# First shift as columns of matmuls, its weights in eight buffers, bias table first

## What is computed

```python
def ada_modulation(c, w, b):
    mod = jax.nn.silu(c) @ w + b            # c: 1024; w: 1024 x 3072
    shift, scale, gate = jnp.split(mod, 3, axis=-1)

# per sublayer m = 0..3 (attention, MLP, pooling, MLP)
h = rms_norm(x, norm_w[m]) * (1.0 + scale) + shift
x = x + gate * sublayer(h)
# attention of sublayer 0: sliding-window scores + bias = rel_bias[t5_bucket(dist)]
```

## Time and profile before

| | us |
|---|---|
| median of three runs | 957.27 (956.63 to 958.10) |
| the profiled execution's own time | 958.09 |
| its span | 956.4 |
| PE busy | 888.4 (93%) |
| DVE busy | 692.1 (72%) |
| ACT busy | 456.8 (48%) |
| first weight matmul starts | 48.44 |
| ACT takes block 0 from PE | 58.22 |

### The profile page before, as it was taken

How to read it: one execution, slowest core, us unless ns; L and a number is a source line. 1 busy time by engine, 2 the same in 40 slices (tenths; PEclk the granted TensorE clock), 3 DMA queues, 4 the chain that set the end, 5 groups by cost and what they waited for, 6 DMA issues and landing times.

```text
span 956.4 us, 17671 instructions
## 1 busy us (share of the span) xinstructions
PE 888.4 (93%) x7028; PEld 852.6 (89%) x7028; DVE 692.1 (72%) x877; ACT 456.8 (48%) x573; POOL 58.0 (6%) x104
## 2 busy tenths in 40 slices
PE   2599999899999996799999999999999999999996
PEld 1388879799999996699999999988989999999996
DVE  4889878788878888766666556855487877776665
ACT  2347464566643333456663433444465444444445
POOL 2110110211111110000000000000000000000000
PEclk9789999999999996799999999999999999999998
DMA  9895755499989994057765555653435555654531
GB/s 336 300 339 193 244 200 177 130 319 322 317 306 330 330 316 134 23 184 234 239 199 176 175 183 168 197 166 130 157 90 177 177 179 187 218 173 158 169 126 44
DMA packets 156600, 196.60 MB, mean 206 GB/s; under 512 B 5341, under 2 KB 143116, under 8 KB 156556
## 3 DMA queue, kind: packets, MB, share of 16 engines
q1 hardware_dynamic: 142732, 145.64, 47.6%
q0 software_dynamic: 13824, 50.34, 14.4%
HBM read 194.90 MB, written 1.06 MB: 205 GB/s over the span
## 4 chain that ended last, share of the span: by engine, by line
PE 81%; DVE 9%; ACT 4%; issue 2%; DMA 2%; SPq 1%; DVEq 0%; ACTq 0%
PE G L557 15%; PE G L558 15%; PE G L559 15%; PE A L557 7%; PE A L559 7%; PE A L558 7%; DVE w_lo L1123 2%; ACT w_hi L1786 2%; PE G L632 2%; PE A L685 2%; PE G L633 2%; PE G L634 2%; DMA sinks<-in_attn_sinks_dram 1%; DMA MIX<-bias_rows 1%; DVE HN L1285 1%
## 5 line engine op out<-in xcount | busy, mean ns | idle before, releaser
L1123 DVE TENSOR_TENSOR w_lo<-raw,w_hi 128x2048 fp32r<-128x2048 f32 x135 | 307.1, 2275 | 163.7 <-ACT w_hi L1786 163.5
L1786 ACT ACTIVATE w_hi<-raw 128x2048 fp32r<-128x2048 f32 x135 | 256.6, 1901 | 265.7 <-PE A L559 132.4
L557 PE MATMUL G<-h_hi,w_hi 128*128 128x256 f32 x880 | 257.9, 293 | 22.5 <-DVE h_lo L1268 13.0
L558 PE MATMUL G<-h_lo,w_hi 128*128 128x256 f32 x880 | 253.3, 288 | 0.0
L559 PE MATMUL G<-h_hi,w_lo 128*128 128x256 f32 x880 | 253.2, 288 | 0.0
L557 PEld LDWEIGHTS G<-h_hi,w_hi 128*128 128x128 f32 x880 | 173.0, 197 | 29.5 <-issue 22.5
L558 PEld LDWEIGHTS G<-h_lo,w_hi 128*128 128x128 f32 x880 | 173.6, 197 | 0.2 <-issue 0.2
L559 PEld LDWEIGHTS G<-h_hi,w_lo 128*128 128x128 f32 x880 | 173.2, 197 | 0.0
L557 PE MATMUL A<-u_hi,w_hi 128*128 128x256 f32 x512 | 143.4, 280 | 0.7 <-DVE w_lo L1123 0.7
L558 PE MATMUL A<-u_lo,w_hi 128*128 128x256 f32 x512 | 142.9, 279 | 0.0
L559 PE MATMUL A<-u_hi,w_lo 128*128 128x256 f32 x512 | 142.9, 279 | 0.0
(11 more groups left out here) (325 smaller groups left out, 1315.7 us busy)
## 6 DMA issues: line engine op xcount, KB each, us to landing
raw<-in_mlp_w_dram SPq DMA_DIRECT2D x64, 1024.0 KB, 5.5
ada_raw<-in_ada_w_dram POOLq DMA_DIRECT2D x88, 512.0 KB, 5.7
raw<-in_w_in_dram SPq DMA_DIRECT2D x14, 1024.0 KB, 5.0
raw<-in_w_up_dram SPq DMA_DIRECT2D x11, 1024.0 KB, 5.4
raw<-in_w_gate_dram SPq DMA_DIRECT2D x11, 1024.0 KB, 5.3
raw<-in_attn_w_in_dram SPq DMA_DIRECT2D x9, 1024.0 KB, 7.1
raw<-in_w_down_dram SPq DMA_DIRECT2D x8, 1024.0 KB, 5.2
raw<-in_attn_w_out_dram SPq DMA_DIRECT2D x4, 1024.0 KB, 5.4
```

Of the source, the lines that this page charges most:

```text
L557: pe.matmul(dst, wh, ah, start=start, stop=False)
L558: pe.matmul(dst, wh, al, start=False, stop=False)
L1123: dve.tensor_tensor(w_lo[n % 2][:, 0:k, :], raw[n % RAW][:, 0:k, :], w_hi[n % 2][:, 0:k, :].bitcast(F32), ALU.subtract).then_inc(lo_done, 1)
L1786: act.activation(w_hi[n % 2][:, 0:k, :], raw[n % RAW][:, 0:k, :], ACT.Copy).then_inc(hi_done, 1)
```

## The change

The shift's weights of sublayer 0 no longer go through DVE. POOL loads them into eight buffers that the opening doesn't use otherwise (`shift_w`), in between and behind the scale's; PE multiplies each 128 x 128 tile by a column of silu(c) and accumulates over the eight k-tiles in one bank (`shift_tile`). `rb` is loaded ahead of x, the table is made before x is turned, stored right behind the vector loads and read back as soon as it is stored. The gate's weights are loaded when block 1 has landed. All other thirds are summed as columns (`add_sums`, which takes a list of thirds), `turn_sums` and its reductions are gone; the first gate's columns move from the attention stage to its end. The norm of block 0 gets a buffer for all eight tiles (`HN0`); ACT makes the copies to BIAS before `g_hi` and w_hi of block 0, and starts the high part when the shift has been read.

```diff
-    return (1, 0, 2)[t // DT], t % DT
+    return (1, 2)[t // DT], t % DT
...
-ADA_B, ADA_C, ADA_D, ADA_E = 24, 40, 64, 88
-ADA_EARLY = (3, 4, 5, 6, 7, 8, 19, 20)
+ADA_B, ADA_C, ADA_D, ADA_E, ADA_ALL = 16, 32, 56, 80, 88
+ADA_EARLY = (3, 4, 5, 6, 7, 11, 12)
...
+        shift_w = [b[:, :, :].rearrange("p t s -> p (t s)") for b in (Q4, K4, V4, GV)] + [
+            PT[:, :, :, :].rearrange("p a b s -> p (a b s)"),
+            wide[:, 4:6, :].rearrange("p a b -> p (a b)"), wide[:, 6:8, :].rearrange("p a b -> p (a b)"),
+            SS[:, :, :, :].rearrange("p a b s -> p (a b s)")]
...
+        HN0 = wide[:, 0:4, :].rearrange("p a (t s) -> p (a t) s", t=2)
...
# SP
                 sp.dma_start(vrows[0:DT, 3, :], c[0].rearrange("(t p) -> t p", p=P)).then_inc(c_in, 16)
+                sp.dma_start(rb[:, :], rel_bias).then_inc(rb_in, 16)
...
                     sp.dma_start(vrows[at:at + count, slot, :], r).then_inc(vecs_in, 16)
-                sp.dma_start(rb[:, :], rel_bias).then_inc(small_in, 16)
+                bank_was_read(sp, "table")
+                sp.dma_start(scratch.ap(), t8[:, :]).then_inc(table_out, 16)
...
-                bank_was_read(sp, "table")
-                sp.dma_start(scratch.ap(), t8[:, :]).then_inc(table_out, 16)
-                load(N_ATTN, w_in[:, :, ATTN_COLS[0]:ATTN_COLS[0] + COLS])
                 sp.wait_ge(table_out, 16)
-                sp.wait_ge(ada_used, 10)
                 sp.dma_start(hankel[:, :, :],
                              bass.AP(scratch, 0, [[1, P], [HANKEL, HEADS], [1, S]])).then_inc(table_in, 16)
+                load(N_ATTN, w_in[:, :, ATTN_COLS[0]:ATTN_COLS[0] + COLS])
+
+                sp.wait_ge(shift_full[DT - 2], 16)
                 for j, col in enumerate(ATTN_COLS[1:], 1):
                     if j < RAW:
-                        sp.wait_ge(ada_used, (14, 16, 16)[j - 1])
+                        sp.wait_ge(ada_used, (5, 7, 8)[j - 1])
...
# POOL
+            def load_shift(k):
+                pool.dma_start(shift_w[k], ada[0][:, k, SHIFT * D:(SHIFT + 1) * D]).then_inc(shift_full[k], 16)
+
+            for scales, shifts in (((0, 1), (0,)), ((2, 3), (1,)), ((4, 5), (2,)), ((6, 7), (3, 4, 5, 6, 7))):
+                for f in scales:
+                    load_first(f)
+                for k in shifts:
+                    if k == DT - 1:
+
+                        pool.wait_ge(table_out, 16)
+                    load_shift(k)
+
+            pool.wait_ge(raw_full[1], 16)
+            for f in range(DT, ADA_B):
+                load_first(f)
...
# PE
+            def add_sums(name, thirds, blocks):
+
+                dst = bank_empty(pe, name)
                 pe.wait_ge(ada_used, blocks)
...
+                for n, (m, part) in enumerate(thirds):
+                    for t in range(DT):
+                        last = pe.matmul(dst[:, DT * n + t:DT * n + t + 1],
+                                         sums_of(m, part)[:, part, t * P:(t + 1) * P],
+                                         ones[:, 0:1], start=True, stop=True)
+                bank_done(name, last)
...
+            def shift_tile(k):
+
+                pe.wait_ge(shift_full[k], 16)
+                for t in range(DT):
+                    last = pe.matmul(shift_dst[:, t:t + 1], shift_w[k][:, t * P:(t + 1) * P],
+                                     c_silu[:, k:k + 1], start=k == 0 and t == 0, stop=k == DT - 1,
+                                     skip_group_check=True)
+                return last
+
+            pe.wait_ge(rb_in, 16)
+            bank_done("table", pe.matmul(bank_empty(pe, "table")[0:HEADS, 0:P], rb[:, :],
+                                         C[0:32, C_HOT:C_HOT + P], start=True, stop=True))
+            bank_was_read(pe, "c")
             pe.wait_ge(x_in, 16)
-            turn_x(0)
-            turn_x(1)
+            for q in range(4):
+                turn_x(q)
+            shift_tile(0)
             pe.wait_ge(vecs_in, 16 * 13)
...
             bank_done("ms0", last)
-            turn_sums(0, "scale", DT)
+            shift_tile(1)
             pe.wait_ge(table_in, 16)
             for q in range(4):
                 dst = bank_empty(pe, f"flip{q}")
                 bank_done(f"flip{q}", pe.matmul(halves(dst), anti, hankel[:, 2 * q:2 * q + 2, :],
                                                 start=True, stop=True))
-            turn_sums(0, "shift", 2 * DT)
+            shift_tile(2)
+            shift_tile(3)
+            add_sums("scale0", ((0, SCALE),), DT)
+            for k in range(4, DT):
+                last = shift_tile(k)
+            bank_done("shift0", last)
...
-            turn_sums(0, "gate", ADA_B)
...
             weighted(0, 7)
+            add_sums("gate0", ((0, GATE),), ADA_B)
...
-            scale_and_shift(1)
+            add_sums("sums1", ((1, SHIFT), (1, SCALE)), ADA_C)
...
-            scale_and_shift(3)
+            add_sums("sums3", ((3, SHIFT), (3, SCALE)), ADA_E)
...
-            turn_sums(3, "gate", 96)
+            add_sums("gate3", ((3, GATE),), ADA_ALL)
...
# DVE
+            def thirds(name, m, first, count):
+
+                at = 3 * DT * m + DT * first
+                src = bank_full(dve, name)
+                bank_read(name, dve.tensor_tensor(
+                    MOD[:, :, :].rearrange("p m n -> p (m n)")[:, at:at + DT * count], src[:, 0:DT * count],
+                    V[:, V_ADAB + at:V_ADAB + at + DT * count], ALU.add))
+                bank_was_read(dve, name)
...
-            chain(part(0, "scale"))
-            factor(0)
             split_lo(0)
-            ada_next(4)
-            part(0, "shift").then_inc(mod_ready, 1)
-            dve.wait_ge(mod_ready, 1)
+            thirds("scale0", 0, SCALE, 1)
+            chain(factor(0))
             ssq[0] = 4
-            norm("n0", 0, GAIN[:, 0, :], MOD[:, 0, 0:DT])
+            dve.wait_ge(rstd_ready, 1)
+            for p in range(4):
+                for t in (2 * p, 2 * p + 1):
+                    ins = dve.scalar_tensor_tensor(out=HN0[:, t, :], in0=X[:, t, :], scalar=GAIN[:, 0, t:t + 1],
+                                                   in1=rstd[:, :], op0=ALU.mult, op1=ALU.mult)
+                ins.then_inc(norm_ready, 1)
+            thirds("shift0", 0, SHIFT, 1)
+            for p in range(4):
+                dve.wait_ge(norm_ready, p + 1)
+                low_pair("n0", p, HN0[:, 2 * p:2 * p + 2, :], shift=MOD[:, 0, 0:DT])
             split_lo(1)
...
-            chain(part(0, "gate"))
...
             gate_of(1)
+            thirds("gate0", 0, GATE, 1)
             low_pair("mix0", 3, MIX[:, 6:8, :], position=1)
...
# ACT
-            act.wait_ge(glr_in, 16)
-            act.activation(g_hi[:, :, :], g_raw[:, :, :], ACT.Copy).then_inc(g_split, 1)
-            split_hi(0)
             root(0)
             for q in range(4):
                 src = bank_full(act, f"flip{q}")
                 bank_read(f"flip{q}", act.activation(BIAS[:, 2 * q:2 * q + 2, :], halves(src), ACT.Copy))
-            act.wait_ge(mod_ready, 1)
-            high_norm("n0", MOD[:, 0, 0:DT])
+            act.wait_ge(glr_in, 16)
+            act.activation(g_hi[:, :, :], g_raw[:, :, :], ACT.Copy).then_inc(g_split, 1)
+            split_hi(0)
+            bank_was_read(act, "shift0")
+            for p in range(4):
+                act.wait_ge(norm_ready, p + 1)
+                for t in (2 * p, 2 * p + 1):
+                    ins = act.activation(h_hi[:, t, :], HN0[:, t, :], ACT.Identity, bias=MOD[:, 0, t:t + 1])
+                ins.then_inc(hhi_ready, 1)
```

More of the change, by code:

```diff
@@ L43, in first_block @@
 def first_block(t):
-    return (1, 0, 2)[t // DT], t % DT
+    return (1, 2)[t // DT], t % DT
 SHIFT, SCALE, GATE = 0, 1, 2
-ADA_B, ADA_C, ADA_D, ADA_E = 24, 40, 64, 88
-ADA_EARLY = (3, 4, 5, 6, 7, 8, 19, 20)
-ADA_SLOT = [1 if f >= ADA_E else f % 3 for f in range(96)]
-ADA_LOADS = [sum(ADA_SLOT[e] == ADA_SLOT[f] and e not in ADA_EARLY for e in range(f + 1)) for f in range(96)]
+ADA_B, ADA_C, ADA_D, ADA_E, ADA_ALL = 16, 32, 56, 80, 88
+ADA_EARLY = (3, 4, 5, 6, 7, 11, 12)
+ADA_SLOT = [1 if f >= ADA_E else f % 3 for f in range(ADA_ALL)]
+ADA_LOADS = [sum(ADA_SLOT[e] == ADA_SLOT[f] and e not in ADA_EARLY for e in range(f + 1)) for f in range(ADA_ALL)]
 def ada_before(f):
@@ L741, in _ @@
             bank_done("vecs", last)
-            pe.wait_ge(small_in, 64)
-            bank_done("table", pe.matmul(bank_empty(pe, "table")[0:HEADS, 0:P], rb[:, :],
-                                         C[0:32, C_HOT:C_HOT + P], start=True, stop=True))
-            turn_x(2)
-            turn_x(3)
             dst = bank_empty(pe, "ms0")
@@ L919, in _ @@
             up(0)
-            add_sums(1, "gate", ADA_D - 2)
+            add_sums("gate1", ((1, GATE),), ADA_D - 2)
             down(0)
-            add_sums(2, "scale", ADA_D)
+            add_sums("scale2", ((2, SCALE),), ADA_D)
             mean_square(2)
-            add_sums(2, "shift", ADA_D)
-            add_sums(2, "gate", ADA_E)
```

(22 more changed lines are left out.)

89 lines of the change are left out of this document (26 added, 63 removed).

## The result

The kernel after takes 991.59 us (median of 4 runs, 988.81 to 993.56) against 957.68 of the kernel before beside it: ratio 1.0352, 95% interval 1.0321 to 1.0384. The direction was forecast, the size was not: 991.6 lies above the range of 963 to 984. The profiled execution took 990.16 us with a span of 988.5, 32.1 more than before's 956.4.

The account below looks back on a forecast made before the run. TensorE, busy 93% of the span, was taken to bound the kernel, so delays of block 0 reach the end. Opening +14.0 and later edits +6.3 make +20.3 on 958.09, 978.4, or 977.6 against the median; given as 977, range 963 to 984.

Parts of the forecast that it names:

- The opening: Up to block 0's end: table at 34.0, flips, seven column groups mostly at half clock, first matmul at 64.2; +14.0 us.
- Rival 1: Opening columns run at the upper clock: seven groups take 12.9 us, opening +3.8, later edits +4.6, 966.5 us; chance 0.21.
- Rival 2: Half clock from the flips to the pool stage, table at 36.9: opening +20.8, later edits +9, 987 us; chance 0.08.
- 3: Rival: bias table comes early, round trip done at 24, block 0 7.6 us earlier, 955.1 us in all; chance 0.04.
- 4: Rival: no difference, table near 26 or columns in a single pass at 0.92 us a group, 958 us; chance 0.04.
- the later edits: Behind the opening, each third once transposed is summed as a column; sum +6.3 us, including -0.9 for transposes leaving attention.
- the second norm: Ahead of its mean square, 16 transposes of about 1.9 us become two column groups of 3.7 us: +1.8.
- my rule of the opening: Behind the flips, the clock holds for two column groups at 1.84 us, then falls: five at 3.56, 21.5 us together.
- the fourth: Fourth modulation's shift and scale: 1.91 us of transposes become columns of 3.7 to 7.1 us; +1.8 to +5.2, taken as +3.5.
- The gate at the end of attention: First gate's columns, 1.84 us right behind the attention outputs, with DVE waiting for them: +1.1.
- these four terms: Column sums of the first gate +1.1, second modulation +1.8, fourth modulation +3.5 and its gate +0.8.
- the fourth gate: Gate of the fourth modulation: 1.06 us of transposes becomes 1.84 us of columns, +0.8.

Follow-up runs that it names:

- experiment 8: Kernel after with 32 unused bytes, scale and shift ahead of the flips, shift weights streamed past silu(c): 964.95 us; with before's transposes, addresses and sum order behind the opening: 953.81 us.
- Experiment 4: Kernel after's opening, with the kernel before's transposes, addresses and order of sums behind it: 973.64 us, ratio 1.0137 to the kernel before.
- experiment 7: Kernel after with 32 unused bytes, TensorE taking shift tiles 2 to 7 and the scale's columns ahead of the table wait and flips, DVE and ACT reordered: 974.65 us.
- experiment 3: Kernel before with only the later sums as columns of matmuls, opening and addresses unchanged: 968.0 us, ratio 1.0100.

## Why the prediction was right and where it was wrong

**The opening held.** The table landed at 33.4 (forecast 34.0), flips 6.69 (6.4), seven groups from 39.96 to 61.17, 21.2 (21.5), 2.3 to the first matmul (2.3), block 0 in 7.5 (8.0). The clock fell in the second group already, the first on its own at 1.84. DVE and ACT lay hidden, with 16.18 us of idle DVE. Rival 1, the upper clock, falls with the windows at 0.50; no run has its case, and experiment 8, with another order and product, is the nearest to it. Rival 2 had the clock but not the size, and 3 and 4 fall with a table at 33.4 and with 16 records a group. Experiment 4 has 13.2 for the opening in its trace and 14.4 in its median, the forecast's term. That each part came within half a microsecond is in part luck: the same opening put the first weight matmul anywhere from 60.45 to 64.74 in six traces. What I didn't see is that the loss lay in the order: the columns stood behind the flips while PE was idle ahead of them (experiment 7).

**The step that failed: the later edits as a swap of durations.** For the second norm I replaced 16 transposes by two groups of columns at the full clock, 3.7 us, "+1.8", and put nothing on the mean square behind them. By my rule of the opening (full clock for two groups, then half) two groups would stay at full clock. Measured: 4.80 us for the two, because the clock fell within them, and the mean square behind them at half clock, 3.8 in place of 1.9: +2.7 + 1.9 = +4.6. For the fourth I took "+3.5", all of it for the columns. They took 4.42 (+2.5), less than that, and the mean square behind them 6.25 us from 420.01 to its end in place of 3.7: +4.9 together. The gate at the end of attention, "1.84 us", took 3.48 at a clock of 0.57, +3.1 where I had +1.1; there the clock was as low without columns (experiment 4), so most of this excess isn't shown to be theirs. Together +13.7 for these four terms (the fourth gate +1.1) where I had +7.2. In experiment 4, with transposes in these places, the second norm lost 0.9 and the fourth nothing; experiment 3 shows the loss with before's opening.

**The terms that were missing.** I read the diff for what it adds and removes on the engines, and not for what it does to addresses. The removal of a 32-byte tile cost 5.0 us in the trace and 8 to 9 in the medians, the largest error of a single term. And I passed over DVE's sums being spread anew in attention: +1.35 in the trace, up to 4.3 in another; a worth in the median isn't shown.

In all: 20.3 forecast; +6.5 by the later edits, +5.0 by the place, +1.35 by the order, -1.2 by the opening make 32.0, the 32.1 measured.

## What to carry to other kernels

In this kernel groups of matmuls that load a full tile of weights for each column kept TensorE busy while its clock fell, and the matmuls behind them paid too: price such groups at half clock from the second or third one on, with what follows them. Turn the product round, so that the large operand streams, or put the columns where the engine would wait anyway: here that alone took back the opening's loss in the trace, and 8 to 9 us in the medians. After a change to the list of tiles, compare the spacing of the untouched matmuls first: here a 32-byte scratch tile was worth as much as the reordering that the change was about. And a term can be right alone and the forecast wrong: what is found for one place has to be priced at every place with the same operation, and for what stands behind it.

## What the runs showed of the hardware

- One-column f32 matmuls with 128 x 128 weights: eight take 1.84 us at 2.4 GHz and 3.55 at 1.2; with 32 columns 1.87 and 3.60. Streaming the same 128 x 1024 block past one column takes 1.88 us in its four records at 2.4 GHz, and weight loads (PEld) are busy for 1.20 of 6.90 us there.
- The granted clock was 0.50 with PE busy 7.00 of 7.00 us in columns, and 1.00 with PE busy 13.47 of 14.00 in streamed rows. The Trainium skill (TensorE: Matmul & The Clock Gate, Part 1) ties the clock to how busy PE has been; read as PE's busy share, the first of these stretches disagrees with it, and the second agrees.
- Back-to-back three-product matmuls of 256 columns start every 120 ns where moving operand and weights have the same address modulo 256, and every 117 ns where the moving one stands 32 bytes behind. At 64, 96 and 160 bytes it was 118, 120 and 118.5.
- Openings that don't differ in their instructions vary by 3 to 4 us: first weight matmul at 60.45 to 64.74 in six traces with the new opening, 46.16 to 49.29 in seven with the old one. In the quickest of the six the four flips took 5.14 us and the clock fell in the third group of columns; in the kernel after they took 6.69 and it fell in the second.
